# The last chunk of an MLP: VectorE adds the banks to the accumulator itself, with the gate in the second weights

## The reference

```python
# cvec is c for the latent tokens and c_ctx for the context tokens
sh1, sc1, g1, sh2, sc2, g2 = _adaln(cvec, p["w_ada"], p["b_ada"])
...
x = x + g1 * mix.astype(x.dtype)
h = _rmsnorm(x, p["norm_mlp"]) * (1 + sc2) + sh2
f = jnp.square(jax.nn.relu(jnp.dot(h, p["w_mlp1"])))      # 1024 -> 4096
x = x + g2 * jnp.dot(f, p["w_mlp2"]).astype(x.dtype)       # 4096 -> 1024
...
y_prompt = _rmsnorm(xp, norm_out)
y_sample = _rmsnorm(xs, norm_out)
```

## Time and profile before

| | |
|---|---|
| three runs | 1334.11, 1334.27, 1331.54 us; median 1334.11 us |
| profiled execution | 1332.0 us, its span 1330.1 us |
| TensorE busy (of the span) | 1218.0 us (92%) |
| VectorE busy | 851.3 us (64%) |
| GpSimd busy | 469.1 us (35%) |
| ScalarE busy | 331.4 us (25%) |
| TensorE clock granted, mean | 0.966 of full speed |

### The profile page before, as it was taken

One profiled execution on the slowest core, in us unless ns is written; L12 is line 12 of the kernel. 1 busy time (PEld: TensorE's weight loads), 2 busy tenths in 40 slices (PEclk: granted clock), 3 DMA queues, 4 the chain that ended last, 5 costly groups with the idle time before them and its releaser, 6 DMA issues.

```text
span 1330.1 us, 18585 instructions
## 1 busy us (share of the span) xinstructions
PE 1218.0 (92%) x6479; PEld 1057.5 (80%) x6479; DVE 851.3 (64%) x1337; ACT 331.4 (25%) x610; POOL 469.1 (35%) x386
## 2 busy tenths in 40 slices
PE   3778989694799899999999999999999999999994
PEld 0178988463597688898898899899899899899893
DVE  2988596999788367745645655655654654654648
ACT  2373424222333367220120121121121121121023
POOL 1100001140000052427436536536536536535636
PEclk9979999797889899999999999999999999999998
DMA  8915244596531123101201101201201101110004
GB/s 187 305 33 105 53 93 132 160 224 167 136 99 66 48 80 111 64 33 32 63 32 32 63 32 32 63 32 32 63 32 32 63 32 32 63 33 30 32 0 142
DMA packets 80009, 101.63 MB, mean 76 GB/s; under 512 B 25506, under 2 KB 62534, under 8 KB 79716
## 3 DMA queue, kind: packets, MB, share of 16 engines
q1 hardware_dynamic: 57744, 80.59, 20.7%
q0 software_dynamic: 4944, 17.08, 4.3%
q10 hardware_dynamic: 17284, 3.47, 1.3%
HBM read 89.53 MB, written 9.49 MB: 74 GB/s over the span
## 4 chain that ended last, share of the span: by engine, by line
PE 79%; DVE 6%; DMA 4%; issue 3%; ACT 3%; POOL 2%; ACTq 1%; SPq 1%; POOLq 0%; DVEq 0%
PE bank L1298 23%; PE bank L1300 23%; PE bank L1299 23%; DMA raw<-in_w_ada 2%; POOL acc L498 2%; PE bank L1311 1%; PE bank L1486 1%; PE bank L1485 1%; ACTq L512 1%; PE bank L1420 1%; PE bank L1402 1%; PE bank L1344 1%; PE bank L1484 1%; DVE x_lo L936 1%; ACT x_hi L542 1%
## 5 line engine op out<-in xcount | busy, mean ns | idle before, releaser
L498 POOL TENSOR_TENSOR acc<-acc,gated 128x512 f32<-128x512 f32 x288 | 401.5, 1394 | 400.5 <-DVE gated L1262 361.5
L1298 PE MATMUL bank<-x_hi,w_hi 128*128 128x384 f32 x960 | 324.5, 338 | 4.1 <-issue 2.7
L1300 PE MATMUL bank<-x_hi,w_lo 128*128 128x384 f32 x960 | 322.3, 336 | 0.0
L1299 PE MATMUL bank<-x_lo,w_hi 128*128 128x384 f32 x960 | 322.0, 335 | 0.0
L1262 DVE TENSOR_TENSOR gated<-bank,gate_b 128x512 f32<-128x512 f32 x288 | 194.2, 687 | 118.5 <-PE bank L1300 104.6
L1298 PE MATMUL bank<-w_hi,f_hi 128*128 128x512 f32 x576 | 224.4, 390 | 1.8 <-DVE w_lo L1243 1.2
L1300 PE MATMUL bank<-w_hi,f_lo 128*128 128x512 f32 x576 | 224.4, 390 | 0.0
L1299 PE MATMUL bank<-w_lo,f_hi 128*128 128x512 f32 x576 | 224.3, 389 | 0.0
L822 ACT ACTIVATE relu<-bank 128x384 f32<-128x384 f32 x96 | 47.2, 493 | 649.4 <-PE bank L1300 646.4
L1252 DVE TENSOR_TENSOR f_tmp<-relu 128x384 f32<-128x384 f32 x96 | 65.2, 680 | 212.4 <-ACT relu L822 212.4
L1298 PEld LDWEIGHTS bank<-x_hi,w_hi 128*128 128x128 f32 x960 | 181.1, 189 | 8.7 <-issue 7.0
(11 more groups left out here) (298 smaller groups left out, 1417.6 us busy)
## 6 DMA issues: line engine op xcount, KB each, us to landing
raw<-in_w_mlp SPq DMA_DIRECT2D x64, 512.0 KB
raw<-in_w_ada SPq DMA_DIRECT2D x48, 512.0 KB
x_tile<-in_x_sample POOLq DMA_DIRECT2D x8, 512.0 KB, 8.8
raw<-in_w_in SPq DMA_DIRECT2D x8, 512.0 KB
raw<-in_w_out SPq DMA_DIRECT2D x8, 512.0 KB
x_again<-in_x_sample POOLq DMA_DIRECT2D x8, 512.0 KB, 3.8
out<-acc SPq DMA_DIRECT2D x8, 512.0 KB, 2.6
u_rows<-proj ACTq DMA_DIRECT2D x4, 576.0 KB, 4.9
```

Of the source, the lines that this page charges most:

```text
L498: GP.tensor_tensor(a, a, BT[i % 4][:], ALU.add).then_inc(s.acc, 1)
L1298: mm(out, sh_, mh, start=first, stop=False)
L1299: mm(out, sh_, ml, start=False, stop=False)
L1300: return mm(out, sl, mh, start=False, stop=last)
```

## The change

It touches only chunk 15, the last one. Four things change there.

VectorE multiplies the two raw tiles of second weights by the latent gate before they are split (`w2_gated`, two operations of 128x1024), and the high part and the remainder are made from these. The blocks of the eight latent tiles then come out of TensorE with the gate already in them, and VectorE adds each bank to `acc` in one operation. GpSimd has no work left in the chunk.

The context tile needs another gate. After `hidden` has used the first weights for the last time, ScalarE and VectorE split the raw second weights once more, ungated, into the buffers of the first weights (`w_hi_51`, `w_hi_52`, `w_lo_55`, `w_lo_56`); blocks 16 and 17 use them, and VectorE multiplies these two banks by the context gate and adds them itself.

`final` of tile t moves one pair of blocks ahead: it stands behind the adds of tile t + 1, where it stood behind the gates of tile t + 2. Since `w2_gated` lies where the `gated` buffers lie, VectorE waits before the chunk until GpSimd has made its last add of chunk 14. TensorE's loop ends one chunk earlier and chunk 15 is straight code.

```diff
+    W2G = [at(f"w2_gated{i}", [P, D], R_A + (24 + 4 * i) * KBYTE) for i in range(2)]
...
-        with gp.Fori(0, NFC) as ch:
+        with gp.Fori(0, NFC - 1) as ch:
...
+        def act_final_chunk():
+            ch = NFC - 1
+            for i in range(6):
+                if i in (2, 3):
+                    act.wait_ge(s.w2_gated, i - 1)
+                    act.wait_ge(s.mm_dve, ch * 18 + B_STRAIGHT)
+                    S.activation(w_split_bufs(W1 + i)[0][:], W2G[i - 2][:], ACT.Copy).then_inc(s.w_hi, 1)
+                relu_out(ch, i)
+            for i in range(2):
+                act.wait_ge(s.mm_act, ch * 6 + (A_STRAIGHT + 6))
+                S.activation(w_split_bufs(W1 + i)[0][:], RAW[(FIRST_MLP + 2 + i) % 4][:], ACT.Copy).then_inc(s.w_hi, 1)
...
+        def final_chunk():
+            ch = NFC - 1
+            dve.wait_ge(s.acc, ADDED + ch * 18)
+            for i in range(6):
+                if i in (0, 1):
+                    n = FIRST_MLP + 2 + i
+                    dve.wait_ge(raw_in[n % 4], ch * 16 + 16 * (n // 4 + 1))
+                    tt(W2G[i][:], RAW[n % 4][:], GBT[:, 0, :], ALU.mult).then_inc(s.w2_gated, 1)
+                square(ch, i)
+                if i in (3, 4):
+                    hi, lo = w_split_bufs(W1 + i - 1)
+                    dve.wait_ge(s.w_hi, ch * 4 + (W1 + i))
+                    tt(lo[:], W2G[i - 3][:], hi[:].bitcast(F32), ALU.subtract).then_inc(s.w_split, 1)
+            for i in range(16):
+                a = ACC[:, i // 2, (i % 2) * 512:(i % 2) * 512 + 512]
+                dve.wait_ge(s.mm_dve, ch * 18 + (B_STRAIGHT + i + 1))
+                tt(a, a, BANK[(6 + i) % 4][:], ALU.add).then_inc(s.acc, 1)
+                if i in (1, 2):
+                    hi, lo = w_split_bufs(W1 + i - 1)
+                    dve.wait_ge(s.w_hi, ch * 4 + (W1 + 4 + i))
+                    tt(lo[:], RAW[(FIRST_MLP + 1 + i) % 4][:], hi[:].bitcast(F32), ALU.subtract).then_inc(s.w_split, 1)
+                if i >= 3 and i % 2 == 1:
+                    final(i // 2 - 1)
+            for n in range(2):
+                a = ACC[:, TT - 1, n * 512:n * 512 + 512]
+                dve.wait_ge(s.mm_dve, ch * 18 + (B_STRAIGHT + 16 + n + 1))
+                tt(BT[n][:], BANK[(6 + 16 + n) % 4][:], GBT[:, 1, n * 512:n * 512 + 512], ALU.mult).then_inc(s.gated_ctx, 1)
+                dve.wait_ge(s.gated_ctx, n + 1)
+                tt(a, a, BT[n][:], ALU.add).then_inc(s.acc, 1)
...
-        chunk(NFC - 1, last=True)
+        final_chunk()
...
+        def back_final():
+            ch = NFC - 1
+            pe.wait_ge(s.w_split, ch * 4 + (W1 + 4))
+            for i in range(18):
+                t, n = i // 2, i % 2
+                pe.wait_ge(s.f_ready, ch * 6 + 2 * (t // 3 + 1))
+                if i < 4:
+                    pe.wait_ge(s.ev_act, ch * 6 + (A_STRAIGHT + 3 + i))
+                else:
+                    pe.wait_ge(s.acc, ch * 18 + (ADDED + i - 3))
+                if i == 16:
+                    pe.wait_ge(s.w_split, ch * 4 + (W1 + 6))
+                for r in range(2):
+                    wh, wl = w_split_bufs(W1 + (2 if t < L else 0) + r)
...
-        with pe.Fori(1, NFC) as ch:
+        with pe.Fori(1, NFC - 1) as ch:
             pe.wait_ge(s.w_split, ch * 4 + (W1 + 2))
             hidden(ch, range(6))
             back(ch)
+        pe.wait_ge(s.w_split, (NFC - 1) * 4 + (W1 + 2))
+        hidden(NFC - 1, range(6))
+        back_final()
```

More of the change, by code:

```diff
@@ L199, in build @@
              "mix_hi", "mix_pool", "mix_ready", "acc", "f_ready", "fin_mm", "fin_ready", "fin_out", "no_in",
-             "y_final", "out_w", "tabs", "ada0", "sqr"]
+             "w2_gated", "gated_ctx", "y_final", "out_w", "tabs", "ada0", "sqr"]
     sem = {n: nc.alloc_semaphore(n) for n in names}
@@ L813, in w_hi_loop, with relu_out, act_chunk @@
             S.activation(w_split_bufs(w)[0][:], RAW[n % 4][:], ACT.Copy).then_inc(s.w_hi, 1)
-        def act_chunk(ch, last=False):
+        def relu_out(ch, i):
+            act.wait_ge(s.mm_act, ch * 6 + (A_STRAIGHT + i + 1))
+            if i >= 2:
+                act.wait_ge(s.f_ready, ch * 6 + (i - 1))
+            S.activation(RL[i % 2][:], BANK[i % 4][:, 0:TG], ACT.Relu).then_inc(s.ev_act, 1)
+        def act_chunk(ch):
             for i in range(6):
@@ L818, in act_chunk @@
                     w_hi_loop(ch, i, 0)
[L819 to L825, removed]
+                relu_out(ch, i)
+            for i in range(2):
+                w_hi_loop(ch, i, 1)
+        def act_final_chunk():
[5 more added lines that the diff above has]
+                    S.activation(w_split_bufs(W1 + i)[0][:], W2G[i - 2][:], ACT.Copy).then_inc(s.w_hi, 1)
+                relu_out(ch, i)
+            for i in range(2):
+                act.wait_ge(s.mm_act, ch * 6 + (A_STRAIGHT + 6))
+                S.activation(w_split_bufs(W1 + i)[0][:], RAW[(FIRST_MLP + 2 + i) % 4][:], ACT.Copy).then_inc(s.w_hi, 1)
         with act.Fori(0, NFC - 1) as ch:
             act_chunk(ch)
-        act_chunk(NFC - 1, last=True)
+        act_final_chunk()
         for t in range(TT):
@@ L1264, in _, with chunk @@
         dve.wait_ge(s.gb_in, 32)
-        def chunk(ch, last=False):
+        def chunk(ch):
             for i in range(6):
@@ L1272, in chunk @@
                 gate(ch, i)
-                if not last and i in (2, 6):
+                if i in (2, 6):
                     lo_loop(ch, 0 if i == 2 else 1, 1)
-                if last and i >= 5 and i % 2 == 1:
-                    final(i // 2 - 2)
+        def final_chunk():
[27 more added lines that the diff above has]
+                tt(a, a, BT[n][:], ALU.add).then_inc(s.acc, 1)
         def final(t):
@@ L1596, in back @@
                 last.then_inc(s.mm_dve, 1)
+        def back_final():
[12 more added lines that the diff above has]
+                    wh, wl = w_split_bufs(W1 + (2 if t < L else 0) + r)
+                    last = three(BANK[(6 + i) % 4][:], (FH[:, r, t * P:(t + 1) * P], FL[:, r, t * P:(t + 1) * P]),
+                                 (wh[:, n * 512:n * 512 + 512], wl[:, n * 512:n * 512 + 512]), r == 0, r == 1)
+                last.then_inc(s.mm_dve, 1)
         pe.wait_ge(s.w_split, W_OUT2 + N_HALF)
```

## The result

The changed kernel takes 1325.68 us (median of 5 runs, 1323.04 to 1327.05) where the kernel before takes 1332.76 us (5 runs of the same comparison, 1331.36 to 1334.27). The ratio is 0.9944, with a 95% interval of 0.9931 to 0.9958: some 7.4 us faster. The profiled execution is the slowest of the five (1327.05 us, span 1325.2 us). It comes to chunk 15 2.5 us later than the profiled execution of before, and nothing ahead of chunk 15 was changed, so the spans alone would show 4.9 us.

A forecast was written before the change was run, and what follows sets the result against it. TensorE bounds up to about 1288 us, then a tail chained through GpSimd's adds. Moving the last scaling from 1323.25 to 1315.73 gains 7.5 us, from the 1334.11 median to 1326.6; range 1323.5 to 1330.5.

The forecast's parts named there:

- The walk: VectorE followed through chunk 15's new order: last scaling begins at 1315.73 instead of 1323.25, 7.5 us gained.
- The pair of 2.58 us: Chunk 15, second half: two adds, reciprocal and scaling hold VectorE 2.58 us per pair of blocks, against 2.72 on TensorE.
- the scaling of 1.28: VectorE's output scaling without GpSimd beside it: instruction 1.285 us, taken as 1.20 after overlap; bounds 1.20 and 2.29.
- The two remainders and the context's two operations: VectorE, second half of chunk 15: remainders of 1.14 us each, context product and add, counted as costs within the 7.5 us.
- The first half: Chunk 15 before the adds: VectorE's later start and two gate products cost nothing; 2.7 us without idle time as cover.
- the removed jump: TensorE's loop end: by the skill's rule one fetch given back, priced 2.7 us, sum about 10; prediction added nothing.
- The stall: Rival at TensorE's loop exit: one wait for code at 1262 us, 2.7 us; gain 4.8, time 1329.3; chance 0.08.
- the code on demand: Rival in chunk 15: code behind the loop comes piecewise, 2.7 us each; slower by 3.3 at four, 1337.4; chance 0.03.
- the longer pair: Rival on VectorE in chunk 15: operations 0.08 us longer, a pair 2.9 us; gain 5.3, time 1328.8; chance 0.07.
- the slow scaling: Rival on VectorE: something other than GpSimd slows the scaling, a pair costs 3.67; time 1335, no change; chance 0.06.
- The small waits of VectorE for TensorE from block 15 on: Expected sign late in chunk 15: VectorE catches up, so add 15 waits for its bank until 1309.32.
- a pace 0.15 us a block slower: GpSimd's adds against TensorE's 1.36 us a block: slower by 0.15 us in any chunk, not caught up in the last.

The follow-up runs named there:

- the kept-busy GpSimd: Changed kernel plus 18 GpSimd adds of 128x512 on unused raw tiles in the last chunk, nobody waiting; ratio to the kernel before 1.0010, stretch 62.07 us.
- the scalings later: Changed kernel with each scaling one pair of blocks later, where the kernel before had it; ratio to the kernel before 0.9953, stretch 54.62 us.

## Why the prediction was right

The forecast was 1326.6 us and a gain of 7.5; measured were 1325.68 us and 7.4 (ratio), 7.44 in the stretch.

**What bounds.** GpSimd was the end of the chain, by its own pace and by its collision with the scalings. Both are shown apart: the collision is 5.5 us of GpSimd's adds when the scalings leave VectorE, and 8.6 us of the stretch (62.07 - 53.47) when GpSimd's adds alone are put back.

**The walk.** All starts of the changed kernel lie 2.54 us later, since its chunk 15 did. With that taken off, the first scaling starts at 1294.55 (forecast 1294.54), the context's product at 1311.33 (1311.30), and the last scaling at 1315.81 (1315.73). The last matmul is at 1311.62; the prediction says "near 1311.9", but its own walk, with block 17 ready at 1312.04 and 0.42 us from a matmul's start to that, gives 1311.62. The pair of 2.58 us and the scaling of 1.28, which were the terms between distant bounds, are what the rows show. The two remainders and the context's two operations cost what was put in for them.

**The first half.** VectorE's first operation waited until 1268.42 on that clock (forecast 1268.3) and the delay reached nobody: TensorE has no wait there.

**The code.** The two packets of q8 cost nothing: TensorE has no wait in chunk 15. The rule of the Trainium skill ("Runtime: NRT & Kernel Launch", section "Instruction fetch mechanics") that a taken branch out of a two-page window makes the engine fetch first would have the removed jump give back a fetch, as the prediction says. This trace shows no such fetch: q8 is silent through the loop's later turns, and the step from the last matmul of chunk 14 to the first of chunk 15 is 0.23 us over the jump (1262.11 to 1262.34 before) and no longer than that without it (1264.66 to 1264.88 in the changed kernel). So there were no 2.7 us to give back. Whether the loop's start lies within that window, where the rule asks for no fetch, no run here shows. The rule's other half, that code is fetched ahead, agrees with the first packet, 1.9 us before the chunk's first matmul. A kernel with nothing but the straight code was not run; that it costs nothing rests on these traces.

**The rivals.** The stall and the code on demand fall with TensorE's gapless matmuls, the longer pair with the 2.58 us, the slow scaling with the 1285 ns; there the kept-busy GpSimd shows that it is GpSimd and neither the stores nor ScalarE that slows it. My row for it had not told ScalarE and GpSimd apart, as the prediction said.

**What was off.** The small waits of VectorE for TensorE from block 15 on are hardly there: two adds at 1311.24 take 1.31 us instead of 1.28.

The prediction gives GpSimd a pace 0.15 us a block slower than TensorE's "in any chunk". Its own pace is 0.07 slower (1.43 against 1.36, with the scalings on ScalarE). In chunk 14 two of the 18 adds took 2.09 us and the others about 1.29, and those two lie beside the remainders of the weights, which VectorE makes from two tiles in SBUF; I read them as the same collision. So the collision is a larger part of GpSimd's lag than the prediction has it. The sum does not use this figure, since GpSimd is gone in the changed kernel.

That the median is only 0.9 us under the forecast is in part luck. The forecast counts from 1334.11; the kernel before, with two more runs, is at 1332.76, and 7.5 us less is 1325.3. Single runs of the changed kernel spread over 4 us. What bears the forecast out is the walk within the chunk, to 0.1 us.

## What to carry to other kernels

A last stage that has no later work to hide its slower engine is worth a look of its own: read the chain there, and divide each engine's time a block by that of the engine it follows. Taking an engine out of a step helps only if the one that takes over keeps the pace; here that needed the second operation to be moved into the weights, where it is done once on 2 tiles instead of on 16 blocks and lies in idle time. What stands last in the program also sets the tail's transfers: a tile with one large store at the end is 2.5 us shorter than one with eight small ones.

## What the runs showed of the hardware that was not expected

The stretch repeats far better than the time: 53.47 us twice, 52.14 and 52.13, while these four executions reach chunk 15 anywhere between 1260.81 and 1266.15 us. The 738 us ahead of it repeat as well: from the last transpose of the output projection's stage (524.6 us before, 527.1 changed, 521.3 with the scalings later) to the first matmul of chunk 15 there are 737.7 to 737.8 us in each, and from the first transpose of that stage (475.7, 478.2 and 472.4 us) 786.6 to 786.7. So the scatter between these executions is made in the first 480 us. Most of TensorE's waits lie there, for weights and for other engines; which of them scatters was not looked into.

An engine that nobody waits for can cost another its whole gain: 18 idle adds on GpSimd made VectorE's operations with two SBUF operands slower by 1.0 us each or less (scalings 1.285 to 2.29, remainders 1.22 to 1.71 and 1.82, the context's adds 0.69 to 1.03). It reached TensorE, too: from the chunk's first matmul to its last there are 52.55 us instead of 49.28, and the view of waits puts 1.6 us of that down to VectorE's adds from the banks.
